# Decoder layer with a mixture of experts: the gate product on the unnormed residual, and the gather's sample rows beside the bias rows

## The reference

```python
h = h + mixed @ w_out
hn = rms_norm(h, norm_ffn)
logits = hn @ w_router + b_router            # 32 experts, top 4, softmax over the four
for e in range(32):
    hdn = hn @ w_up[e] + b_up[e]             # 1024 x 2048
    gt, up = min(hdn[:, :1024], 7), clip(hdn[:, 1024:], -7, 7)
    acc += gates[:, e] * (((up + 1) * gt * sigmoid(1.702 * gt)) @ w_down[e] + b_down[e])
h = h + acc
gate = sigmoid(rms_norm(h, norm_ple) @ w_ple_gate)      # 1024 x 1024
h = h + gate * (p @ w_ple_proj)
y = rms_norm(h, norm_final)
```

## Time and profile before

| | |
|---|---|
| median of 3 runs | 1230.79 us (1230.73, 1230.79, 1236.77) |
| profiled execution, its own time | 1228.1 us |
| its span, first to last instruction | 1226.3 us |
| PE busy | 1152.9 us, 94% of the span |
| weight load of PE | 494.1 us, 40% |
| VectorE busy | 330.3 us, 27% |
| ScalarE busy | 189.8 us, 15% |
| GpSimd busy | 80.2 us, 7% |
| HBM read | 436.65 MB, 358 GB/s over the span |

### The profile page before, as it was taken

The page is one execution under the profiler, slowest core; times in us unless marked ns, Lnnn a source line. Parts: engine busy times, 40 slices in busy tenths (PEclk is TensorE's granted clock), DMA queues, the critical chain, the costliest instruction groups (busy, mean ns, idle before and its releaser), DMA issues.

```text
span 1226.3 us, 14536 instructions
## 1 busy us (share of the span) xinstructions
PE 1152.9 (94%) x5741; PEld 494.1 (40%) x5741; DVE 330.3 (27%) x597; ACT 189.8 (15%) x367; POOL 80.2 (7%) x137
## 2 busy tenths in 40 slices
PE   4997898999999999999999999999999999999884
PEld 3664543333333333333333443333333333333364
DVE  5999332121112111111121111112221112112133
ACT  3144321101011010101011111011111011010022
POOL 4664000000000000000000000000000000000000
PEclk9996898999999999999999999999999999999888
DMA  9431524999999999999999999999999999999800
GB/s 297 159 117 61 189 96 185 424 429 428 428 427 429 428 428 428 429 429 429 428 429 429 426 428 427 420 428 427 429 428 429 428 428 428 427 428 427 342 1 35
DMA packets 46428, 438.68 MB, mean 358 GB/s; under 512 B 11056, under 2 KB 15280, under 8 KB 21024
## 3 DMA queue, kind: packets, MB, share of 16 engines
q1 hardware_dynamic: 45760, 437.59, 85.2%
q10 hardware_dynamic: 624, 0.45, 0.1%
HBM read 436.65 MB, written 2.41 MB: 358 GB/s over the span
## 4 chain that ended last, share of the span: by engine, by line
PE 67%; DMA 23%; DVE 6%; ACT 2%; issue 1%; ACTq 0%; DVEq 0%; SPq 0%
PE ps L1068 27%; DMA ring_up<-in_w_up_dram 23%; PE ps L1086 12%; PE ps L1040 4%; PE ps L1004 4%; PE ps L1292 2%; PE ps L785 2%; PE ps L1058 2%; PE ps L586 1%; PE ps L1206 1%; PE ps L1050 1%; PE ps L1075 1%; DVE ps L1749 1%; PE ps L641 1%; PE ps L920 1%
## 5 line engine op out<-in xcount | busy, mean ns | idle before, releaser
L1068 PE MATMUL ps<-ring_up,region 128*64 128x512 f32 x2048 | 451.1, 596 | 10.1 <-DMA ring_up<-in_w_up_dram 10.1
L1068 PEld LDWEIGHTS ps<-ring_up,region 128*64 128x64 f32 x2048 | 143.7, 137 | 293.2 <-issue 271.6
L1086 PE MATMUL ps<-ring_dn,region 128*64 128x512 f32 x1024 | 229.0, 599 | 0.4 <-ACT region L1557 0.4
L2081 DVE TENSOR_SCALAR region<-ps 128x512 f32<-128x512 f32 (+1 forms) x33 | 22.6, 684 | 459.0 <-PE ps L1068 445.4
L1086 PEld LDWEIGHTS ps<-ring_dn,region 128*64 128x64 f32 x1024 | 70.8, 137 | 132.6 <-issue 128.3
L2075 DVE TENSOR_TENSOR fb<-fb,ps 128x528 f32<-128x528 f32 x64 | 45.0, 704 | 253.7 <-PE ps L1004 244.7
L1040 PE MATMUL ps<-n_tok,region 128*64 128x512 f32 (+1 forms) x384 | 94.1, 608 | 1.3 <-DVE region L2024 1.3
L1553 ACT ACTIVATE region<-region 128x512 f32<-128x512 f32 x32 | 20.2, 630 | 454.6 <-DVE region L2081 454.6
L1567 ACT ACTIVATE region<-ps 64x512 f32<-64x512 f32 x64 | 37.9, 592 | 246.1 <-PE ps L1086 245.7
L1004 PE MATMUL ps<-region 128*128 128x264 f32 x256 | 74.5, 413 | 0.9 <-DVE fb L2075 0.9
L547 POOL COPY region<-kst 128x64 f32 (+1 forms) x33 | 7.8, 237 | 984.6 <-PE ps L1068 948.2
(11 more groups left out here) (382 smaller groups left out, 820.8 us busy)
## 6 DMA issues: line engine op xcount, KB each, us to landing
ring_up<-in_w_up_dram SPq DMA_DIRECT2D x132, 2048.0 KB, 20.5
ring_dn<-in_w_down_dram SPq DMA_DIRECT2D x66, 2048.0 KB, 18.3
ring_up<-in_w_in_dram SPq DMA_DIRECT2D x4, 1024.0 KB, 10.2
ring_dn<-in_w_out_dram SPq DMA_DIRECT2D x1, 4096.0 KB
ring_up<-in_w_ple_gate_dram SPq DMA_DIRECT2D x4, 1024.0 KB, 20.6
x_tok<-in_x_prompt_dram SPq DMA_DIRECT2D x2, 512.0 KB
ring_up<-in_w_in_dram SPq DMA_DIRECT2D x2, 512.0 KB, 8.7
ring_up<-in_w_glu_dram SPq DMA_DIRECT2D x1, 1024.0 KB
```

What stands on the lines that cost most here:

```text
L1068: m = mm(ps[64 * (q % 2):64 * (q % 2) + 64, HID_B + q // 2, :], xe[:, k % 4, k // 4], ring_up[:, k, q * 512:(q + 1) * 512], start=False, s ...
L1086: m = mm(ps[64 * half:64 * half + 64, OUT_B, :], act_t[:, f % 4, 64 * (f // 4):64 * (f // 4) + 64], ring_dn[:, f, 512 * half:512 * half + ...
L2081: V.tensor_scalar(gl, bank(HID_B, n_), LIMIT, None, ALU.min).then_inc(Z["g_rdy"], 1)
```

## The change

Three things are changed, and some code around them.

**Sample rows beside the bias rows.** `gather` keeps only the two prompt chunks. The two matmuls of the sample chunk (8 array rows, 0 to 7) move into `bias_and_samples`, which alternates them with the 4 bias matmuls. The bias rows and the one-hot rows now lie on partitions 64 to 127 (`B_ROW = 64`). The gathered tokens are complete only after this step, so at the start of the experts it stands before `turn_gathered`.

**Gathered rows turned within the down product.** `turn_gathered` moves from before `down` to between its two halves; on ScalarE `gathered` moves behind `activation`.

**The gate product on the unnormed residual.** `added` always adds, so that `fb` ends as the residual itself, transposed. The norm's weights are multiplied into the gate's weights in SBUF, four blocks by GpSimd and four by ScalarE, as soon as they have landed. The product runs on the unnormed `fb`; the sum of squares by token comes from a matmul of ones with `fb` squared, behind block 0; VectorE multiplies each block with the inverse root before the sigmoid. The residual is added in the transposed layout, each block is transposed back by itself two blocks later, and the final norm reads PSUM. The stores go chunk by chunk.

```diff
@@ SP
-                             ).then_inc(ld_gate_w, 16)
+                             ).then_inc(ld_gate[k // 2], 16)
+            for c in range(2):
+                sp.wait_ge(Z["f_out"], c + 1)
+                sp.dma_start(O[0][0, c * P:(c + 1) * P, :], n_tok[:, c]).then_inc(Z["st_y"], 16)
             sp.wait_ge(Z["f_out"], 3)
-            for c in range(2):
-                sp.dma_start(O[0][0, c * P:(c + 1) * P, :], n_tok[:, c]).then_inc(Z["st_y"], 16)
@@ GpSimd, at its end
+            pool.wait_ge(ld_gate[0], 32)
+            for b in range(4):
+                nc.gpsimd.tensor_scalar(w_gate[:, b], w_gate[:, b], vecs[:, V_PLE + b:V_PLE + b + 1], 1.0,
+                                        ALU.mult, ALU.mult).then_inc(Z["wg_rdy"], 1)
@@ PE, gather
-                for c, (t0, nt) in enumerate(CHUNKS):
+                for c in range(2):
                     for half in range(2):
-                        m = mm(ps[64 * half:64 * half + 64, XG_B, :], sel[0:nt, c, a],
-                               n_tok[0:nt, c, 512 * half:512 * half + 512], start=(c == 0), stop=(c == 2))
-                m.then_inc(Z["xg_ps"], 1)
+                        mm(ps[64 * half:64 * half + 64, XG_B, :], sel[:, c, a],
+                           n_tok[:, c, 512 * half:512 * half + 512], start=(c == 0), stop=False)
@@ PE, bias
-            def bias(t):
+            def bias_and_samples(t, a):
                 pe.wait_ge(Z["hot_rdy"], t + 2)
                 for half in range(2):
+                    rows_ = slice(B_ROW + NE * half, B_ROW + NE * half + NE)
                     for q in range(2):
-                        mm(ps[64 * q:64 * q + 64, HID_B + half, :], one_hot[NE * half:NE * half + NE],
-                           b_up[NE * half:NE * half + NE, q * 512:(q + 1) * 512], start=True, stop=False)
+                        mm(ps[64 * q:64 * q + 64, HID_B + half, :], one_hot[rows_], b_up[rows_, q * 512:(q + 1) * 512],
+                           start=True, stop=False)
+                    m = mm(ps[64 * half:64 * half + 64, XG_B, :], sel[0:NB, 2, a],
+                           n_tok[0:NB, 2, 512 * half:512 * half + 512], start=False, stop=True)
+                m.then_inc(Z["xg_ps"], 1)
@@ PE, pair (the second expert of a pair alike)
-                bias(t + 1)
+                bias_and_samples(t + 1, 1)
+                down(t, FIRST)
                 turn_gathered(t + 1)
-                down(t, FIRST)
@@ PE, start of the experts
             gather(0, 0)
+            pe.wait_ge(ld_bup, 32)
+            bias_and_samples(0, 0)
             turn_gathered(0)
-            pe.wait_ge(ld_bup, 32)
-            bias(0)
@@ PE, the end (the transposes back and forth and back() are gone)
+            for o in range(KD):
+                if o >= 2:
+                    pe.wait_ge(Z["gz_lin"], o - 1)
                 for k in range(KD):
+                    if o == 0 and k % 2 == 0:
+                        pe.wait_ge(Z["cmb_read"], (n_visits + PAIRS) * 4 + (k // 2 - 3))
+                    if o == 0 and k == 0:
+                        pe.wait_ge(Z["wg_rdy"], KD)
+                    m = mm(bank(o % 2, T), w_gate[:, k, o * P:(o + 1) * P], fb[:, k, :], start=(k == 0), stop=(k == KD - 1))
+                m.then_inc(Z["gz_ps"], 1)
+                if o == 0:
+                    for k in range(KD):
+                        if k % 2 == 0:
+                            pe.wait_ge(Z["norm_ssq"], 6 + k // 2 + 1)
+                        m = mm(bank(SSQ_B, T), ones, h_square[:, k, :], start=(k == 0), stop=(k == KD - 1))
                     m.then_inc(Z["back_ps"], 1)
+                if o >= 2:
+                    turn_back(o - 2)
+            turn_back(KD - 2)
+            turn_back(KD - 1)
@@ ScalarE, pair
                 gate_values(t)
+                activation(t)
                 gathered(t + 1)
-                activation(t)
@@ ScalarE, the end
+            act.wait_ge(ld_gate[1], 32)
+            for b in range(4, KD):
+                f(w_gate[:, b], w_gate[:, b], ACT.Copy, scale=vecs[:, V_PLE + b:V_PLE + b + 1]).then_inc(Z["wg_rdy"], 1)
+            for j in range(4):
+                act.wait_ge(Z["cmb_read"], (n_visits + PAIRS) * 4 + (j - 3))
+                f(h_square[:, 2 * j:2 * j + 2], fb[:, 2 * j:2 * j + 2], ACT.Square).then_inc(Z["norm_ssq"], 1)
+            f(small[0:1, 103:104], eps[0:1], ACT.Sqrt)
+            act.wait_ge(Z["back_ps"], 2)
+            f(h_rstd, bank(SSQ_B, T), ACT.Sqrt, scale=1.0 / D, bias=eps).then_inc(Z["norm_root"], 1)
+            f(small[0:1, 101:102], eps[0:1], ACT.Sigmoid)
...
+            for o in range(KD):
+                act.wait_ge(Z["gz_lin"], o + 1)
+                f(sg_t[:, o % 2], sg_t[:, o % 2], ACT.Sigmoid).then_inc(Z["gz_sig"], 1)
+                if o == 6:
+                    act.wait_ge(Z["back_ps"], 3)
+                    for c in range(3):
+                        y_squares(c, 0).then_inc(Z["norm_ssq"], 1)
+            f(small[0:1, 102:103], eps[0:1], ACT.Sqrt)
+            act.wait_ge(Z["rstd"], 6)
+            act.wait_ge(Z["back_ps"], 4)
             for c, (t0, nt) in enumerate(CHUNKS):
+                chain(y_squares(c, 1))
+                f(stat[0:nt, c, 2:3], stat[0:nt, c, 3:4], ACT.Sqrt, scale=1.0 / D, bias=stat[0:nt, c, 1:2]
+                  ).then_inc(Z["norm_root"], 1)
@@ VectorE, the end
+            dve.wait_ge(Z["norm_root"], 7)
+            chain(V.reciprocal(h_rstd, h_rstd))
             dve.wait_ge(Z["pp_sb"], KD)
             for o in range(KD):
+                dve.wait_ge(Z["gz_ps"], o + 1)
+                V.tensor_tensor(sg_t[:, o % 2], bank(o % 2, T), h_rstd, ALU.mult).then_inc(Z["gz_lin"], 1)
                 dve.wait_ge(Z["gz_sig"], o + 1)
-                V.tensor_tensor(fa[:, o, :], fa[:, o, :], sg_t[:, o % 2], ALU.mult).then_inc(Z["gz_mul"], 1)
+                chain(V.tensor_tensor(fa[:, o, :], fa[:, o, :], sg_t[:, o % 2], ALU.mult))
+                V.tensor_tensor(fa[:, o, :], fa[:, o, :], fb[:, o, :], ALU.add).then_inc(Z["gz_mul"], 1)
```

More of the change, by code:

```diff
@@ L1151, in pair @@
                 turn_activations(t + 1)
+                if place != "last":
+                    bias_and_samples(t + 2, 0)
+                down(t + 1, FIRST)
                 if place == "last":
@@ L1154, in pair @@
                 else:
-                    bias(t + 2)
                     turn_gathered(t + 2)
-                down(t + 1, FIRST)
                 if place == "embed":
@@ L1589, in pair @@
                     gathered_visit(0)
-                else:
+                activation(t + 1)
+                if place != "last":
                     gathered(t + 2)
-                activation(t + 1)
                 if place == "embed":
@@ L2070, in added @@
                     acc, out = fb[:, 2 * j:2 * j + 2], ps[:, b_:b_ + 2, 0:T]
-                    if isinstance(n_, int) and n_ == 0:
-                        V.tensor_copy(acc, out).then_inc(Z["cmb_read"], 1)
-                    else:
+                    if not isinstance(n_, int) or n_ > 0:
                         dve.wait_ge(Z["cmb_read"], 4 * n_ + j - 3)
-                        V.tensor_tensor(acc, acc, out, ALU.add).then_inc(Z["cmb_read"], 1)
+                    V.tensor_tensor(acc, acc, out, ALU.add).then_inc(Z["cmb_read"], 1)
             def activation(t, n_=512):
```

106 lines of the change are left out of this document (31 added, 75 removed).

## The result

The changed kernel takes 1215.53 us (median of 4 runs, 1214.08 to 1216.75) where the kernel before took 1231.13 beside it: ratio 0.9862, 95% interval 0.9831 to 0.9894. That is 15.6 us less, where 13.1 were forecast (1217.7, range 1213.0 to 1223.0). The profiled execution took 1214.08 us, with a span of 1212.3, 14.0 less than before; the median lies 1.4 us above the profiled execution here, and 2.7 to 3.0 above it before.

A forecast was written before the change was run, and what follows sets the result against it. The weight stream at 428 GB/s was taken to bound the kernel until the last gate weights land, then the end. Terms -0.6, -0.3 and -12.2 gave 1230.8 - 13.1 = 1217.7 us, range 1213.0 to 1223.0.

The forecast's parts named there:

- The middle: no gain from shorter PE work: Experts: PE needs about 27.3 us per expert, below the weight stream's 29.36, so the stream hides any PE saving.
- -0.6 for slice 26: Weight stream: slice 26 shows 420 instead of 428 GB/s behind the embedding experts; a faster PE removes it, -0.6 us.
- The start, -0.3: Start of the experts: bias and samples overlap, so the first `up` starts sooner, -0.3 us, range -0.4 to +0.7.
- Step 1: End: ScalarE scales four gate weight blocks in 4.6 us, to 1165.7; GpSimd's four end between 1165.4 and 1168.4.
- Step 2: End: block 0 of the gate product takes 6.0 us, with 4.1 us at slow clock, to 1171.7.
- Step 4: End: root, reciprocal (1.84 us) and first multiply run beside block 1, done at 1178.0, 0.9 us early for block 2.
- Steps 5 to 7: End: remaining blocks 3.96 us apart to 1202.2, last block's work to 1204.6, final norm's scaling to 1210.1.
- Step 8: End: last store takes 4.0 us instead of 4.8, as two of three stores are issued before; span ends at 1214.1.
- (a): Rival at the product's start: slow GpSimd or clock costs 2.7 + 1.7 us, with a late experts' start 1222.8; 15%.
- (b): Rival in the experts: row groups do not mix, PE needs 31.4 us per expert and becomes the bound, 1282; 4%.
- (c): Rival at the end: almost no gain, stream ends later or each block's chain runs unhidden, 12 us, 1229.7; 5%.
- (d): Rival at the start: `up` starts at full clock, first slots released 1.5 us sooner, 1215.0; 12%.

The follow-up runs named there:

- the middle undone: Changed kernel with the diff's parts on gather, bias, pair, start of the experts and ScalarE's pair taken back, new end kept: 1213.03 us, ratio 0.9876.
- the middle alone: Kernel before with only the parts on gather, bias, pair, start of the experts and ScalarE's pair put in, old end kept: 1229.71 us, ratio 1.0006.
- the stores together: Changed kernel with its three stores of the result all issued behind the last scaling: 1217.30 us, ratio 0.990.
- the ten matmuls: Changed kernel with ten unused matmuls of 264 columns put between the last combination matmul and the gate product: 1217.15 us, ratio 0.9902.
- the wait per block: Changed kernel with the gate product's first output block waiting for each scaled weight block, not all eight: 1213.14 us, again 1213.65 beside 1215.18 unedited.

## Why the prediction was right

*The middle: no gain from shorter PE work.* Right, and shown from both sides by the two kernels with the middle undone and alone. PE's period came to 27.7, not 27.3: the row groups mix (six matmuls in 1.03 us, four in 1.02 before), 1.0 us is saved in the gather, and 0.30 goes back to the wait for VectorE's activation and about 0.2 to turns and `down`. One reading was off and cost nothing: 28.33 is the longer of two periods that alternate (28.33 and 27.96, mean 28.15), so PE was 1.21 us per expert under the stream and not 1.03. What the prediction didn't add up is how short the cover is in total, 8.5 us over 28 experts. For the moved transposes the trace shows `down` in two parts of 3.58 where it had 7.02, 0.14 more, and the four transposes at 0.67 as before. The Trainium skill, TensorEngine Tiling (Array Packing), section Key Properties, has a drain at every change of tiling mode; whatever the added changes cost here is within that 0.14.

*-0.6 for slice 26.* Wrong. The dip is gone from the GB/s row, but the landing came 958.5 us after the first refill, and 957.8 before. What a dip of 8 GB/s in one slice gave back was lost elsewhere; where isn't shown.

*The start, -0.3.* The size is near, and the profiled execution didn't show it. From the gather to the first `up` were 7.13 us before; 7.78 in the profiled execution, whose six matmuls fell into half clock (193.01 to 194.9); 6.70 in the second (188.76 to 195.46), and 6.68 to 6.75 with the same start in the kernels with the middle alone, the stores together, the ten matmuls and the wait per block. The 0.4 that it gives is lost again in the first expert, which the prediction had not seen: the "whole half of `down`" was spare for the gathered rows, but the activation's transposes came to wait.

*The end.* Step 1, ScalarE to 1165.7: 1165.5, and the product at 1165.62. GpSimd took 1.10 us a block, half of the lower bound, and was done at 1160.8. Step 2, 6.0 for block 0: 6.23 from its start to that of the squares' sum (1165.62 to 1171.85), since the clock came back 5.3 us after the start and not 4.1. Step 3: 3.56, as said. Step 4: the reciprocal took 1.80 (1.84 by the line through 157 and 253 ns), the first multiply came at 1177.97 (1178.0 said). Steps 5 to 7: PE's last block to 1202.1 (1202.2), last scaling 1210.07 (1210.1), blocks 3.89 apart (3.96). The root's table was loaded in 1.28 us and the next activation began 0.02 behind it, so the drain of 1.38 that the Trainium skill, ScalarE: Activation LUTs, section What ACT_TABLE_LOAD costs, would add is not there, and the measurement decides.

*Step 8, the store, 4.0 us.* Mis-sized by 1.8. I took 0.8 of issue time out of 4.8. What counted was that the two large stores were under way while the third chunk was scaled, and the third one has 8 rows: 2.2 us. The kernel with the stores together brings the 4.8 back. This one term is the difference between -12.2 and the -14.0 measured.

Of the end's gain, the runs vary by themselves only the stores and the wait for the scaled blocks. That the rest, some 11.4 us, is the 48 transposes and the norm ahead of the product is read from the timelines of before and after.

*How the sum came out so near.* In part by luck. The -0.9 of slice 26 and the start didn't come, the store gave 1.8 more than was said, and the median lies 1.4 us above the profiled execution where 2.7 were taken over from the kernel before. The first two leave the profiled execution 0.9 us under the 1215.0 forecast for it, and with the third the median is 2.2 under 1217.7.

*The rivals.* (a) GpSimd or the clock: refuted for GpSimd, 0.2 us for the clock. (b) the row groups: they mix; on shared rows the price is 0.83 us, and it takes PE above the stream to matter, as the gather's pair done four more times shows. (c) refuted: every multiply is hidden behind a block. (d) the start gains 0.4 us at most, and it is given back.

## What to carry to other kernels

Where a stream and an engine race over a whole phase, compare their totals, with the odd iterations in them, and not one period; a saving on the side that is covered is worth nothing, and a short loss on that side counts where the lead is thin: at the start of the phase and behind the odd iterations. What comes after the last load is paid in full: take work off that path by linearity (scale the weights, normalise the product later), wait for each piece and not for all, and send the large outputs off before the last small one.

## What the runs showed of the hardware that was not expected

- Matmuls of 8 rows (0 to 7) and of 32 (64 to 127, two of them) began within 0.04 us of each other; the six took 1.03 us, and four of them alone 1.02; on common rows the same eight-row matmuls cost 0.83 us per expert.
- GpSimd multiplied 128 x 1024 fp32 in 1.10 us, 1.1 ns a column; its 128 x 256 in the kernel before took 0.556, 2.2 ns a column.
- Between PE's last combination matmul, at the end of the last visit's branch, and its next one lie 2.1 to 3.2 us without a wait that the profile shows (2.14 in the kernel before, 2.51 and 3.18 in two kernels with the wait per block, 2.86 with the ten matmuls). It bounds the product's start once the weights' wait is gone.
- The clock was at the lower level within a microsecond of PE's last combination matmul, so filling the idle time behind it came too late. In the kernel before the 1-us window 1160 to 1161 has 0.55 granted, with PE busy until 1160.7; in the changed kernel it has 0.82 and the next 0.50, with PE busy until 1160.7; in its second execution the fall lies in 1161 to 1162 (0.56), half a microsecond after PE stopped at 1160.5. In the changed kernel PE had been busy for 3.4 of the 5 us from 1156 on.
- An idle time of 1.13 us in the first expert was followed by 1.7 us lost to half clock in 7 of 9 executions, and the stream lost 1.1 to 1.6 us of transfers behind it.
